# Branch sum on VectorE inside each attention-branch tile, earlier loads of the residual rows, and an unrolled output projection with the second norm and the first up tile woven in

## The chip, the cores and the metric

The kernel runs on one core of one Trainium2 chip. The metric is the device time of one execution in microseconds, and the figure quoted is a median over runs. The kernel before takes 1816.24 us (three runs, 1814.94 to 1818.01).

## The reference

One inference step of a decoder layer over 1024 prompt tokens and 8 x 4 sample tokens (1056 rows in all), all in float32. What matters here is the middle of it:

```
h = rmsnorm(x, g_mix_pre); z = h @ w_in            # pooling branch A, attention branch B, two gates
merged = gates[:D] * (pool_out @ w_branch_pool) + gates[D:] * (attn @ w_branch_attn)
x  = x + rmsnorm(merged @ w_out, g_mix_post)       # output projection, post norm, residual
up = rmsnorm(x, g_ffn_pre) @ ffn_w_up              # second norm, then the feed-forward
c  = causal depthwise conv of width 3 over [history, up]
x  = x + rmsnorm((gelu(c[:D_FF]) * c[D_FF:]) @ ffn_w_down, g_ffn_post)
```

D is 1024 and D_FF 2816. Each layer also returns its updated states (pool rows, key and value caches, convolution history).

## The kernel before

The program is written out engine by engine, with semaphores; each engine does its instructions in the order in which they are written, and so do the two queues that issue transfers (SyncE, shown as SPq, and GpSimd's). Nothing is scheduled by a planner.

**Products.** Every float32 product is three passes of TensorE: operands are split into a high part (a copy on ScalarE into a rounded type) and a low part (a subtraction on VectorE), and hi*hi, hi*lo and lo*hi are summed in PSUM. So each weight slice needs a load, a ScalarE copy and a VectorE subtraction before TensorE may use it.

**Layout.** In the projections of the input, of branch B and of the up matrix, channels lie on partitions and the 1056 tokens are three blocks of 352 columns (`BW`). In the output projection the tokens lie on partitions: nine tiles of 128 tokens, each 8 chunks x 3 passes x 2 halves of 512 columns, so 48 matmuls a tile.

**Around the change**, in order of time:
- Branch B's projection (L928 to L947): eight tiles j of 18 matmuls into banks 0 to 2 and 3 to 5 by turns. For tile j VectorE multiplies PSUM by the gate into `sga` (L1653), then makes `wo_lo` for slice j of w_out (L1655). GpSimd adds `sga` to `merged` (L690) and raises `sum_done`. SyncE loads the eight slices of w_out through four buffers `wo_stage` (L568); a buffer is loaded again when its `wo_lo` is done.
- SyncE then waits for all eight `wo_lo` and all eight sums, and issues the residual rows (`xnat`, two loads of 2 MB and two small ones, `load_x`, L441 to L444), the two gains `gpost` and `gb2` (L573, L575; the trace calls the second one gb), and the first weights of the up-projection (L507).
- Output tiles (`out_tile`, L952 to L962): tile n needs `mg_hi` and `mg_lo` of its tokens and, for its PSUM banks, the residual of tile n - 2. ScalarE (`split_merged`, `post_norm`, L1230 to L1245) makes `mg_hi`, squares and sums the PSUM tile into `pjunk`, takes the root, and squares the new `xnat` row. VectorE (`low_merged`, `residual`, L1661 to L1676) makes `mg_lo`, the reciprocal, `ptmp` and the new `xnat`. Six tiles run in loops of two; before its loop VectorE waits for both gains and all of `xnat`.
- Second norm: after tile 7, VectorE takes the reciprocals and scales two rows into `hn2` (L1360), in two buffers. TensorE transposes them (`turn_tiles`, L722 to L737, 8 transposes a tile), ScalarE and VectorE copy the result into `hT_hi` (L1041) and `hT_lo` (L1368), which lie over `wo_hi` and `wo_lo`. Only when all nine tiles are through does GpSimd clear `chist` (L693), after which SyncE loads the convolution history (L586), TensorE transposes it (L984) and starts up tile 0 (`channels`, L825 to L833: 72 matmuls for each of two halves).
- The up-projection has 22 such pairs of halves, then follows the down-projection (L1011).

## Time and profile before

| | |
|---|---|
| device time, median of 3 runs | 1816.24 us |
| span of the profiled execution | 1810.3 us |
| TensorE busy in it | 1655.2 us, 91% |
| VectorE, ScalarE, GpSimd busy | 730.4, 580.0, 184.6 us |
| branch B projection | 807.1 to 831 us |
| output tiles | 841.4 to 949.5 us |
| transposes of the second norm | 954.1 to 977.2 us |
| first half of up tile 0 | 981.0 to about 994.1 us |

The profile gives the span from the first to the last instruction. The profiled execution's own device time is not listed apart: the three runs lie 4.6 to 7.7 us above the span, and that difference, taken here as what lies around the span, is assumed to stay. The granted clock of TensorE is written as a share of 2.4 GHz, so 0.50 is 1.2 GHz.

### The profile page before, as it was taken

What the parts mean: (1) busy time and instruction counts of PE and PEld (TensorE: products, weight loads), DVE (VectorE), ACT (ScalarE), POOL (GpSimd) and SP (SyncE); (2) the same over time, 40 slices, a digit from 0 to 9 for tenths busy, and PEclk for the clock granted to TensorE, in tenths of its full rate; (3) what the DMA queues carried; (4) which work ended last, traced back from release to release, by engine and by line L of the source; (5) the groups of instructions that cost most, each with busy time, mean ns of one, the idle gap of its engine ahead of it and who ended that gap; (6) DMA issues with size and microseconds to landing.
All of it is one profiled execution on the core that took longest, in us unless ns stands there. A gap on an engine that the chain in (4) does not pass through costs nothing.

```text
span 1810.3 us, 26548 instructions
## 1 busy us (share of the span) xinstructions
PE 1655.2 (91%) x9651; PEld 1528.4 (84%) x9651; DVE 730.4 (40%) x1220; ACT 580.0 (32%) x1083; POOL 184.6 (10%) x223
## 2 busy tenths in 40 slices
PE   3999996776889999996996999999999999999996
PEld 2798895776889999995886999999999997878784
DVE  4424325563632223125344444334444344454533
ACT  5221214452322222232332333333333333343432
POOL 0011114444010000005000000000000000000000
PEclk8999997787889999998997999999999999999998
DMA  4232217776123332125002555555562114555542
GB/s 160 94 93 83 79 48 237 236 235 206 30 81 94 93 102 82 47 77 189 3 0 85 170 173 178 176 184 193 193 197 72 60 64 159 177 186 175 187 160 89
DMA packets 146747, 232.89 MB, mean 129 GB/s; under 512 B 13617, under 2 KB 114273, under 8 KB 145928
## 3 DMA queue, kind: packets, MB, share of 16 engines
q1 hardware_dynamic: 134944, 198.99, 34.7%
q0 software_dynamic: 11760, 33.35, 5.0%
q8 instruction: 25, 0.41, 0.1%
q14 instruction: 18, 0.15, 0.0%
HBM read 202.56 MB, written 77.36 MB: 155 GB/s over the span
## 4 chain that ended last, share of the span: by engine, by line
PE 79%; issue 6%; DMA 4%; DVE 3%; POOL 2%; SPq 2%; ACT 2%; POOLq 0%; DVEq 0%; ACTq 0%
PE PS L832 44%; PE PS L1011 14%; PE PS L753 11%; PE PS L959 5%; PE PS L892 2%; POOL merged L690 1%; SPq L520 1%; DMA gb<-in_norm_ffn_pre 1%; PE PS L731 1%; DMA qb<-zs 1%; DVE hn L1360 1%; SPq L515 1%; PE PS L808 1%; POOL qb L665 1%; ACT junk L1049 1%
## 5 line engine op out<-in xcount | busy, mean ns | idle before, releaser
L832 PE MATMUL PS<-hT_hi,tw_hi 128*128 128x352 f32 x1536 | 346.2, 334 | 16.8 <-DVE poolT_lo L1534 7.9
L832 PE MATMUL PS<-hT_hi,tw_lo 128*128 128x352 f32 x1536 | 338.0, 328 | 0.0
L832 PE MATMUL PS<-hT_lo,tw_hi 128*128 128x352 f32 x1536 | 337.9, 329 | 0.0
L832 PEld LDWEIGHTS PS<-hT_hi,tw_hi 128*128 128x128 f32 x1536 | 267.2, 195 | 19.0 <-issue 7.9
L1493 DVE TENSOR_TENSOR tw_lo<-tw_stage,tw_hi 128x1024 fp32r<-128x1024 f32 x74 | 86.2, 1167 | 464.1 <-ACT tw_hi L1140 460.3
L832 PEld LDWEIGHTS PS<-hT_hi,tw_lo 128*128 128x128 f32 x1536 | 270.1, 193 | 0.0
L832 PEld LDWEIGHTS PS<-hT_lo,tw_hi 128*128 128x128 f32 x1536 | 267.9, 193 | 0.0
L1140 ACT ACTIVATE tw_hi<-tw_stage 128x1024 fp32r<-128x1024 f32 x74 | 74.7, 1012 | 263.5 <-PE PS L832 248.9
L1716 DVE TENSOR_TENSOR wd_lo<-wd_stage,wd_hi 128x1024 fp32r<-128x1024 f32 x66 | 80.9, 1225 | 154.1 <-ACT as_hi L1274 153.3
L1739 DVE SCALAR_TENSOR_TENSOR cacc<-cext,cols,cacc 128x1024 f32<-128x1024 f32 x88 | 113.0, 1285 | 65.3 <-ACT cacc L1295 30.3
L1011 PE MATMUL PS<-wd_hi,as_hi 128*128 128x512 f32 x396 | 125.9, 399 | 9.9 <-DVE ytmp L1780 8.1
L1273 ACT ACTIVATE wd_hi<-wd_stage 128x1024 fp32r<-128x1024 f32 x66 | 69.9, 1059 | 176.7 <-PE PS L1011 168.1
L1011 PE MATMUL PS<-wd_lo,as_hi 128*128 128x512 f32 x396 | 124.0, 394 | 0.0
L1011 PE MATMUL PS<-wd_hi,as_lo 128*128 128x512 f32 x396 | 123.8, 394 | 0.0
L1011 PEld LDWEIGHTS PS<-wd_hi,as_hi 128*128 128x128 f32 x396 | 75.1, 192 | 28.3 <-DVE ytmp L1780 10.1
L1011 PEld LDWEIGHTS PS<-wd_lo,as_hi 128*128 128x128 f32 x396 | 75.5, 191 | 16.9
L1011 PEld LDWEIGHTS PS<-wd_hi,as_lo 128*128 128x128 f32 x396 | 75.2, 190 | 16.5
L753 PE MATMUL PS<-wqk_hi,hT_hi 128*128 128x512 f32 x216 | 86.2, 399 | 2.3 <-DVE wqk_lo L1389 2.3
L753 PE MATMUL PS<-wqk_hi,hT_lo 128*128 128x512 f32 x216 | 85.6, 396 | 0.0
L753 PE MATMUL PS<-wqk_lo,hT_hi 128*128 128x512 f32 x216 | 85.3, 395 | 0.0
L1304 ACT ACTIVATE cnat<-PS 18x256 f32<-18x256 f32 x22 | 8.2, 372 | 182.7 <-PE PS L977 182.7
L665 POOL TENSOR_TENSOR qb<-kt,qb 128x1024 f32<-128x1024 f32 x24 | 56.4, 2353 | 64.2 <-DMA qb<-zs 64.0
(235 smaller groups left out, 2361.8 us busy)
## 6 DMA issues: line engine op xcount, KB each, us to landing
wd_stage<-in_ffn_w_down SPq DMA_DIRECT2D x66, 512.0 KB, 3.3
tw_stage<-in_ffn_w_up SPq DMA_DIRECT2D x44, 512.0 KB, 3.9
out_k_s<-in_cache_k_w SPq DMA_DIRECT2D x8, 2044.0 KB
out_v_s<-in_cache_v_w SPq DMA_DIRECT2D x8, 2044.0 KB
qb<-zs SPq DMA_DIRECT2D x24, 512.0 KB, 5.8
acts<-cact POOLq DMA_DIRECT2D x22, 528.0 KB, 8.6
tw_stage<-in_w_in SPq DMA_DIRECT2D x20, 512.0 KB, 5.1
as_stage<-acts SPq DMA_DIRECT2D x44, 192.0 KB, 3.3
```

Of the source, the lines that this page charges most:

```text
L515: sp.dma_start(srow[h:P:NH, g, :, :], zs_s[g, h]).then_inc(s_rows_in, 16)
L665: pool.tensor_tensor(qb[s][:, :, :], k, qb[s][:, :, :], ALU.mult).then_inc(s_prod, 1)
L753: last = pe.matmul(PS[:, bank + n % 3, 0:width], x[:, k, t0:t0 + P], w[:, k, :], start=(k == 0 and j == 0), stop=(k == KC - 1 and j == 2))
L832: last = pe.matmul(PS[:, 3 * s + b, 0:BW], w[s][:, k, :], x[:, k, b * BW:(b + 1) * BW], start=(k == 0 and j == 0), stop=(k == kc - 1 and j ...
L892: last = pe.matmul(PS[0:DH, 6, bass.ds(r + g * P, 1)], vt[g][:, t, h * DH:(h + 1) * DH], sPT[:, g, bass.ds(r, 1)], start=True, stop=True)
L959: last = pe.matmul(PS[:, 2 * s + b, :], x[s][:, k, :], w[:, k, b * 512:(b + 1) * 512], start=(k == 0 and j == 0), stop=(k == KC - 1 and j ...
L1011: mm = pe.matmul(PS[:, 2 * pair + b, :], x[s][:, t0:t0 + P], w[s][:, b * 512:(b + 1) * 512], start=(first and j == 0), stop=(last and j == 2))
L1140: act.activation(tw_hi[s][:, 0:kc, :], tw_stage[s][:, 0:kc, :], ACT.Copy).then_inc(tw_hi_done, 1)
L1273: act.activation(wd_hi[s][:, :], wd_stage[s][:, :], ACT.Copy)
L1493: dve.tensor_tensor(tw_lo[s][:, 0:kc, :], tw_stage[s][:, 0:kc, :], tw_hi[s][:, 0:kc, :].bitcast(F32), ALU.subtract).then_inc(tw_lo_done, 1)
L1716: dve.tensor_tensor(wd_lo[s][:, :], wd_stage[s][:, :], wd_hi[s][:, :].bitcast(F32), ALU.subtract)
L1739: dve.scalar_tensor_tensor(acc[j + 1][:, 0:TP], e[:, lag:lag + TP], w, acc[j][:, 0:TP], ALU.mult, ALU.add)
```

## The change

It does five things.
1. The sum `merged + sga` moves from GpSimd to VectorE, right behind the multiplication of the same tile. Only three of the eight `wo_lo` stay among these tiles (after j = 3, 5 and 6); the other five come after `mg_lo` of tile 0.
2. SyncE issues the first 2 MB of the residual rows between slices 6 and 7 of w_out, as soon as branch B's matmuls are done, then `gpost` (after five sums) and `gb2` (after eight), and the other rows when all `wo_lo` are done. VectorE waits for each part of `xnat` at tiles 0, 4 and 8.
3. ScalarE splits tile 0 of `merged` before the last slice of w_out.
4. The loops over output tiles are written out. ScalarE takes a root per tile for the second norm too, and VectorE scales row n directly behind the residual of tile n, into `merged`, whose columns are free by then (tile 8 into `hn2_last`). TensorE transposes tile 0 behind output tile 7 and tile 1 behind output tile 8.
5. The first half of up tile 0 runs block by block (`up_first`): from the transposes of tile 4 on, three matmuls of block 0 follow each tile's transposes, then the rest of block 0 and blocks 1 and 2. The transposes of the history stand behind it.

```diff
         @block.sync
+                if k == 6:
+                    sp.wait_ge(tp_done[1], PAIR_BA + 1)
+                    load_x(0)
+            sp.wait_ge(sum_done, 5)
+            sp.dma_start(gpost[:, :], ...).then_inc(gain_in, 16)
+            sp.wait_ge(sum_done, KC)
+            sp.dma_start(gb2[:, :], ...).then_inc(gain_in, 16)
             sp.wait_ge(wo_lo_done, KC)
-            sp.wait_ge(sum_done, KC)
-            for a in range(3):
-                load_x(a)
...
+            load_x(1)
+            load_x(2)
         @block.gpsimd
-            for j in range(KC):
-                pool.wait_ge(ba_used, j + 1)
-                pool.tensor_tensor(merged[:, j, :], merged[:, j, :], sga[:, j, :], ALU.add).then_inc(sum_done, 1)
         @block.tensor
             out_tile(0, 0, True)
-            with pe.Fori(0, 4) as i:
-                out_tile(i * 2 + 1, 1)
-                out_tile(i * 2 + 2, 0)
-            pe.wait_ge(o_x2, 9 + 2)
-            turn_tiles(1, hn2)
-            pe.wait_ge(ht_done[1], 9 + 2)
+            for n in range(1, NTILE):
+                out_tile(n, n % 2)
+                if n >= 7:
+                    turn_second(n - 7)
+            pe.wait_ge(tw_lo_done, PAIR_UP * 2 + 1 + 2)
+            def up_first(b, k):
+                for j, (w, x) in enumerate(((tw_hi, hT_hi), (tw_hi, hT_lo), (tw_lo, hT_hi))):
+                    mm = pe.matmul(PS[:, b, 0:BW], w[0][:, k, :], x[:, k, b * BW:(b + 1) * BW], ...)
+                return mm
+            for n in range(2, NTILE):
+                turn_second(n)
+                if n == 4:
+                    pe.wait_ge(ht_done[1], 3 + 2)
+                    pe.wait_ge(o_x2, 9 + 2)
+                if n >= 4:
+                    up_first(0, n - 4)
+            for k in range(5, KC):
+                up_first(0, k)
+            for b in range(1, NBLK):
+                pe.wait_ge(ht_done[1], (3, 6, 9)[b] + 2)
+                for k in range(KC):
+                    last = up_first(b, k)
+            last.then_inc(tp_done[0], 1)
...
-            up(0, True)
+            turn_history(0)
+            channels(PAIR_UP, 1, KC, hT_hi, hT_lo, conv0[1], 0)
             up(1)
         @block.scalar
             split_merged(0, 0, 0)
+            split_wo(KC - 1)
+            for n in range(NTILE - 1):
+                split_merged(n + 1, (n + 1) % 2, LAST if n + 1 == 8 else (n + 1) * P)
                 act.wait_ge(ss_done, n + 9 + 1)
+                post_square(n)
+                second_square(n)
+                if n == 5:
+                    split_tw(PAIR_UP, 0, KC)
+                    split_tw(PAIR_UP, 1, KC)
+            act.wait_ge(ss_done, 8 + 9 + 1)
+            post_square(8)
+            split_turned(1, 0)
+            split_turned(1, 1)
+            second_square(8)
+            for n in range(2, NTILE):
                 split_turned(1, n)
         @block.vector
                 dve.tensor_tensor(g, PS[:, 3 * (j % 2):3 * (j % 2) + 3, 0:BW], g, ALU.mult).then_inc(ba_used, 1)
-                dve.wait_ge(wo_hi_done, j + 1)
-                dve.tensor_tensor(wo_lo[:, j, :], wo_stage[j % 4][:, :], wo_hi[:, j, :].bitcast(F32), ALU.subtract)\
-                   .then_inc(wo_lo_done, 1)
+                dve.wait_ge(ba_used, j + 1)
+                dve.tensor_tensor(merged[:, j, :], merged[:, j, :], sga[:, j, :], ALU.add).then_inc(sum_done, 1)
+                if j in (3, 5, 6):
+                    low_wo((3, 5, 6).index(j))
...
             low_merged(0, 0, 0)
+            for k in range(3, KC):
+                low_wo(k)
+            low_merged(1, 1, P)
             dve.wait_ge(gain_in, 48)
-            dve.wait_ge(x_in[0], 32)
-            dve.wait_ge(x_in[1], 32)
-            dve.wait_ge(x_in[2], 64)
...
+            for n in range(NTILE):
+                if n % 4 == 0:
+                    dve.wait_ge(x_in[n // 4], 64 if n == 8 else 32)
+                residual(n)
+                if n + 2 < NTILE:
+                    low_merged(n + 2, n % 2, LAST if n + 2 == 8 else (n + 2) * P)
+                if n == 6:
+                    low_tw(PAIR_UP, 0, KC)
+                    low_tw(PAIR_UP, 1, KC)
+                if n < 8:
+                    second_norm(n)
+            low(1, 0)
+            low(1, 1)
+            second_norm(8)
+            for n in range(2, NTILE):
                 low(1, n)
```

`turn_second(n)` is eight transposes of row tile n; `post_square`, `second_square`, `residual` and `second_norm` are the bodies of the old steps, one tile each; `residual` no longer waits for the residual before it.

How the instructions stand, at three places. First VectorE from tile 6 of branch B's projection to the output tiles (`sga` is the gated product, the numbers of `wo_stage` its four buffers, those of `mg_lo` the buffers of output tiles 0 and 1). Before:

```order
L1653 TENSOR_TENSOR sga<-PS,sga 128x1056
L1655 TENSOR_TENSOR wo_lo<-wo_stage_181,wo_hi 128x1024
L1653 TENSOR_TENSOR sga<-PS,sga 128x1056
L1655 TENSOR_TENSOR wo_lo<-wo_stage_182,wo_hi 128x1024
L1663 TENSOR_TENSOR mg_lo_185<-merged,mg_hi_183 128x1024
```

Now:

```order
L1690 TENSOR_TENSOR sga<-PS,sga 128x1056
L1692 TENSOR_TENSOR merged<-merged,sga 128x1056
L1681 TENSOR_TENSOR wo_lo<-wo_stage_181,wo_hi 128x1024
L1690 TENSOR_TENSOR sga<-PS,sga 128x1056
L1692 TENSOR_TENSOR merged<-merged,sga 128x1056
L1701 TENSOR_TENSOR mg_lo_185<-merged,mg_hi_183 128x1024
L1681 TENSOR_TENSOR wo_lo<-wo_stage_182,wo_hi 128x1024
L1681 TENSOR_TENSOR wo_lo<-wo_stage_179,wo_hi 128x1024
L1681 TENSOR_TENSOR wo_lo<-wo_stage_180,wo_hi 128x1024
```

The sum stands behind each product, the `wo_lo` behind tile 6 is that of slice 2 instead of slice 6, and those of slices 3 to 7 follow the first `mg_lo`.

Second, SyncE's queue at the same time, now:

```order
L568 DMA wo_stage_181<-in_w_out 128x1024
L441 DMA xnat<-in_x_prompt 128x4x1024
L568 DMA wo_stage_182<-in_w_out 128x1024
L573 DMA gpost<-in_norm_mix_post 128x1024
L575 DMA gb_190<-in_norm_ffn_pre 128x1024
L441 DMA xnat<-in_x_prompt 128x4x1024
```

and before:

```order
L568 DMA wo_stage_181<-in_w_out 128x1024
L568 DMA wo_stage_182<-in_w_out 128x1024
L441 DMA xnat<-in_x_prompt 128x4x1024 x2
L443 DMA xnat<-in_x_prompt 96x1024
L444 DMA xnat<-in_x_sample 32x1024
L573 DMA gpost<-in_norm_mix_post 128x1024
```

One half of the rows went ahead of the last slice of w_out, the other behind both gains.

Third, TensorE behind output tile 8 (`ident,hn` and `ident,merged` are transposes, `ident,chist` those of the history). Before:

```order
L731 MATMUL PS<-ident,hn_194 128x128 x8
L734 REGISTER_ALU
L734 COMPARE_AND_BRANCH
L731 MATMUL PS<-ident,hn_193 128x128 x8
L984 MATMUL PS<-ident,chist 128x128 x2
L832 MATMUL PS<-hT_hi,tw_hi_73 128x352 x3
L832 MATMUL PS<-hT_lo,tw_hi_73 128x352 x3
L832 MATMUL PS<-hT_hi,tw_lo_75 128x352 x3
```

Now:

```order
L958 MATMUL PS<-wo_hi,mg_lo_186 128x512 x2
L967 MATMUL PS<-ident,merged 128x128 x32
L978 MATMUL PS<-hT_hi,tw_hi_73 128x352
L978 MATMUL PS<-hT_lo,tw_hi_73 128x352
L978 MATMUL PS<-hT_hi,tw_lo_75 128x352
L967 MATMUL PS<-ident,merged 128x128 x8
```

The transposes of tiles 1 to 4 follow the last output tile, and behind those of tile 4 stand the first three matmuls of up tile 0 (L978 is `up_first`), where before the history's transposes and all of up tile 0 came last.

## Rows read from the trace of the kernel before

**Rows 1.** The page's first part: busy time, share of the span, instructions.
```profile
PE 1655.2 (91%) x9651; PEld 1528.4 (84%) x9651; DVE 730.4 (40%) x1220; ACT 580.0 (32%) x1083; POOL 184.6 (10%) x223
```

**Rows 2.** The chain of waits, in order of time: start, length, what.
```profile
811.77 27.14 POOL merged L690 x8
...
981.33 24.36 PE PS L832 x144
```

**Rows 3.** Timeline, branch B projection: start, length, engine, line, tiles [idle <-releaser].
```profile
810.13 0.64 PE L941 MATMUL PS<-attnT_hi,tw_hi 128*128 128x352 f32 x3
...
810.43 1.26 DVE L1653 TENSOR_TENSOR sga<-PS,sga 128x1056 f32<-128x1056 f32 x1 [3.35 <-PE PS L941]
...
811.60 1.22 DVE L1655 TENSOR_TENSOR wo_lo<-wo_stage,wo_hi 128x1024 fp32r<-128x1024 f32 x1
...
820.75 2.33 DVE L1655 TENSOR_TENSOR wo_lo<-wo_stage,wo_hi 128x1024 fp32r<-128x1024 f32 x1
...
824.68 0.65 PE L941 MATMUL PS<-attnT_hi,tw_hi 128*128 128x352 f32 x3
...
838.94 1.06 ACT L1232 ACTIVATE mg_hi<-merged 128x1024 fp32r<-128x1024 f32 x1 [11.36 <-POOL merged L690]
```

**Rows 4.** View of the tile merged: durations in ns min/median/max, first and last start.
```profile
L1663 DVE TENSOR_TENSOR mg_lo<-merged,mg_hi x9: 1217/1225/1227, 840.1 to 934.2; 128x1024 fp32r<-128x1024 f32 x9
...
L690 POOL TENSOR_TENSOR merged<-merged,sga x8: 3380/3429/3456, 811.8 to 835.5; 128x1056 f32<-128x1056 f32 x8
```

**Rows 5.** Timeline, output tiles 0 to 2.
```profile
841.42 1.19 PE L959 MATMUL PS<-wo_hi,mg_hi 128*128 128x512 f32 x2 [10.46 <-issue]
...
855.43 1.02 ACT L1237 ACTIVATE pjunk<-PS 128x1024 f32<-128x1024 f32 x1 [13.07 <-PE PS L959]
...
859.20 1.23 DVE L1663 TENSOR_TENSOR mg_lo<-merged,mg_hi 128x1024 fp32r<-128x1024 f32 x1 [17.88 <-DMA gb<-in_norm_ffn_pre]
...
860.48 1.22 PE L959 MATMUL PS<-wo_hi,mg_hi 128*128 128x512 f32 x2 [5.25 <-DVE mg_lo L1663]
```

**Rows 6.** DMA issues between 780 and 1010 us: KB each, median us to landing.
```profile
wo_stage<-in_w_out SPq DMA_DIRECT2D x8, 512.0 KB, 3.5
...
xnat<-in_x_prompt SPq DMA_DIRECT2D x2, 2048.0 KB, 12.2
...
gb<-in_norm_ffn_pre SPq DMA_DIRECT2D x1, 512.0 KB, 17.3
```

**Rows 7.** Stretches: busy (x) of PE, PEld, DVE, ACT, POOL; PEclk, DMA share, GB/s.
```profile
841.40:846.70 5.30, 5.28 (x13) 4.14 (x14) 0.00 (x0) 0.96 (x1) 0.00 (x0) 0.50 1.00 389
...
953.80:960.00 6.20, 4.02 (x18) 3.65 (x19) 2.85 (x3) 3.49 (x5) 0.00 (x0) 0.50 0.00 0
...
983.50:993.50 10.00, 10.00 (x63) 10.00 (x63) 0.00 (x0) 0.00 (x0) 0.00 (x0) 1.00 0.88 304
```

**Rows 8.** Timeline, last output tiles, transposes and first up-projection.
```profile
884.42 1.03 ACT L1237 ACTIVATE pjunk<-PS 128x1024 f32<-128x1024 f32 x1 [2.41 <-PE PS L959]
...
949.56 1.02 ACT L1237 ACTIVATE pjunk<-PS 128x1024 f32<-128x1024 f32 x1 [5.14 <-PE PS L959]
...
952.55 1.23 DVE L1676 TENSOR_TENSOR xnat<-xnat,ptmp 128x1024 f32<-128x1024 f32 x1
...
954.12 3.65 PE L731 MATMUL PS<-ident,hn 128*128 128x128 f32 x16 [4.59 <-DVE xnat L1676]
...
956.09 1.02 ACT L1041 ACTIVATE hT_hi<-PS 128x1024 fp32r<-128x1024 f32 x1 [0.80 <-PE PS L731]
...
957.15 1.23 DVE L1368 TENSOR_TENSOR hT_lo<-PS,hT_hi 128x1024 fp32r<-128x1024 f32 x1 [3.37 <-ACT hT_hi L1041]
...
965.16 1.09 PE L731 MATMUL PS<-ident,hn 128*128 128x128 f32 x8 [1.57 <-DVE hn L1360]
...
980.67 0.66 PE L984 MATMUL PS<-ident,chist 128*128 128x128 f32 x2 [3.46 <-issue]
...
994.15 1.06 ACT L1140 ACTIVATE tw_hi<-tw_stage 128x1024 fp32r<-128x1024 f32 x1 [16.52 <-PE PS L832]
```

More of the change, by code:

```diff
@@ L237, in build @@
         assert sb.end() <= V
-        hn2 = [at(Y + 4 * D * (1 + 2 * s))(f"hn2{s}", [P, D]) for s in range(2)]
+        hn2_last = at(Y + 3 * 4 * D)("hn2_last", [P, KC, P])
         CW_ = 2 + TP + NB * 6
@@ new lines, in post_square, with second_square @@
+                act.wait_ge(o_ss, n + 1)
+                act.activation(prms[:, 0, n:n + 1], pss[:, 0, n:n + 1], ACT.Sqrt, bias=eps[:, 0:1],
+                               scale=1.0 / D).then_inc(o_rms, 1)
+            def second_square(n):
+                act.wait_ge(o_x2, n + 1 + 2)
+                act.activation(pjunk[:, :], xnat[:, n, :], ACT.Square, accum_out=ss[:, 1, n:n + 1]).then_inc(ss_done, 1)
+                act.wait_ge(ss_done, n + 9 + 1 + 1)
+                act.activation(rms[:, 1, n:n + 1], ss[:, 1, n:n + 1], ACT.Sqrt, bias=eps[:, 0:1],
+                               scale=1.0 / D).then_inc(rms_done[1], 1)
@@ L1645, in _, with low_wo @@
             dve.wait_ge(sga_done, 4 + 1)
+            def low_wo(k):
+                dve.wait_ge(wo_hi_done, k + 1)
+                dve.tensor_tensor(wo_lo[:, k, :], wo_stage[k % 4][:, :], wo_hi[:, k, :].bitcast(F32), ALU.subtract)\
+                   .then_inc(wo_lo_done, 1)
             for j in range(KC):
@@ L1675, in residual, with second_norm @@
                 dve.wait_ge(o_step, n * 2 + 2)
-                dve.tensor_tensor(row, row, ptmp[:, :], ALU.add).then_inc(o_x2, 1)
+                dve.tensor_tensor(xnat[:, n, :], xnat[:, n, :], ptmp[:, :], ALU.add).then_inc(o_x2, 1)
+            def second_norm(n):
+                dve.wait_ge(rms_done[1], n + 1)
+                dve.reciprocal(rstd[:, 1, n:n + 1], rms[:, 1, n:n + 1]).then_inc(rstd_done[1], 1)
+                dve.wait_ge(rstd_done[1], n + 1)
+                if n == 8:
+                    dve.wait_ge(o_mm, NTILE + 2)
+                dst = hn2_last[:, :, :] if n == 8 else merged[:, :, n * P:(n + 1) * P]
+                dve.scalar_tensor_tensor(dst, xnat[:, n, :].rearrange("p (c d) -> p c d", d=P), rstd[:, 1, n:n + 1],
+                                         gb2[:, :].rearrange("p (c d) -> p c d", d=P),
+                                         ALU.mult, ALU.mult).then_inc(hn_ready[1], 1)
```

86 lines of the change are left out of this document (28 added, 58 removed).

## The prediction

> **What bounds the kernel now.** The page's first part [rows 1] has TensorE busy for 1655.2 of 1810.3 us, so only TensorE's idle or slowly clocked time can be won. The chain of waits tells where that is: from 981.33 on it is matmuls without a gap, 24.36 us for 144 of them, the pace of the whole up-projection; just before the output projection GpSimd's eight sums hold it for 27.14 us [rows 2]. The timeline shows three more places between 811 and 994 us, all in the code that the diff touches: TensorE waits 10.46 us before output tile 0, 5.25 us before tile 1 [rows 5], and from the last output tile (949.56) to the end of the first half of up tile 0 (994.15) 44.6 us pass [rows 8] for 72 transposes and 72 matmuls that take some 21 at full clock (nine times 1.09 [rows 8], and half of 24.36 less the cold start). Whatever ends the first half earlier moves all behind it by as much, because up and down run at TensorE's pace and their loads are issued by the same relative waits.
>
> **1. Branch B's sum, to the first output tile.** Each of the eight tiles takes TensorE (824.68 - 810.13) / 5 = 2.91 us [rows 3]. GpSimd takes 3.43 us per sum [rows 4] and ends last: ScalarE's `mg_hi` had waited 11.36 us for it and began at 838.94 [rows 3]. On VectorE, the multiplication takes 1.26 us at 1056 columns and `wo_lo` 1.22 at 1024 when GpSimd is idle, 2.33 when it adds at the same time [rows 3]; the nine `mg_lo`, of the same form and with GpSimd idle, all take 1.22 to 1.23 [rows 4]. So I price the sum on VectorE at 1.22 * 1056 / 1024 = 1.26 (bounds: 1.2 from `mg_lo`, 2.4 if 2.33 were the cost of the place and not of GpSimd; then the eight sums and three `wo_lo` would end at 846.7, and tile 0 would start 9 us later). I take the lower, since the row at 811.60 is the same instruction at the same place. The Trainium skill, SBUF — State Buffer, section "SBUF: two separate sides", says that VectorE with two SBUF inputs and GpSimd exclude each other for a whole instruction. By that rule, the trace agrees (1.22 against 2.33), and 1.26 holds now that GpSimd adds nothing; against it the sum below would be 9 us smaller.
> VectorE now needs 2.52 us a tile against TensorE's 2.91, plus 1.22 for `wo_lo` behind tiles 3, 5 and 6. Walked through from 810.43 [rows 3]: tile 3 starts at 819.05, `wo_lo` 0 ends 823.0, `wo_lo` 1 at 829.4, `wo_lo` 2 at 833.2, and the last sum at 835.8, 3 us earlier than GpSimd's. But ScalarE does `wo_hi` of slice 6 ahead of `mg_hi`, and slice 6 is issued only when `wo_lo` 2 is done: 833.2 + 3.5 to land [rows 6] + 1.06 = 837.8. Then `mg_hi` 1.06 and `mg_lo` 1.23: tile 0 starts at 840.3 instead of 841.42. **Gain 1.1 us** (bounds: 2.5 if slice 6 were no hindrance; -3 if the 2 MB of `xnat` issued right behind slow it).
> Slice 7 is the next to be late: its `wo_lo` 3 comes after `mg_lo` 0, so it is issued at 841.6, behind the 2 MB of `xnat` issued at 833.7. 3.5 us when alone, up to 17.3 as `gb2` had behind 5 MB [rows 6]. The two large loads landed in 12.2 us each by the median, two of them overlapping [rows 6], so one should be through in some 7 to 8, and I take 4.5: wo_lo 7 is done at about 849. Tile 0 took 14.0 us (841.42 to 855.43 [rows 5]), because TensorE starts it at half clock (granted 0.50 for 5.3 us [rows 7]); its last eighth begins some 12 us in, at 852.5. Hidden, with 3.5 us of cover.
>
> **2. Tile 1 and the pace.** Before, VectorE stood 17.88 us before `mg_lo` 1 because the gains and all of `xnat` came first, and TensorE stood 5.25 us [rows 5] and then ran at half clock again for 3.6 us (8 matmuls at 0.43 instead of 0.23: 1.6 us). Now `mg_lo` 1 stands ahead of that wait, done at about 850, 4 us before tile 0 ends. The gains (issued 842.6, 1.5 MB in the queue) should be there by 850; they are first wanted at 855.8. Tile 2 onwards: from one `pjunk` to the next 10.86 us pass, (949.56 - 884.42) / 6 [rows 8], all TensorE. ScalarE and VectorE need after a tile's end: square 1.2, root 0.3, reciprocal 0.2, `ptmp` 1.3, `xnat` 1.2 (949.56 to 953.78 with the pauses [rows 8]), second square and root 1.5, `mg_hi` 1.06, `mg_lo` 1.23, so 8.2 us, within 10.86; at n = 5 the two weight splits on ScalarE make it 10.3, still within. VectorE's second norm (0.2 + 1.3 a tile) fits beside it. So the tiles run gapless: 94.13 us from `pjunk` 0 to `pjunk` 8 [rows 5, 8] become 8 * 10.86 + 1.1 for tile 0's transposes (1.09 at full clock [rows 8]) = 88.0. **Gain 6.1 us.** Tile 8 ends at 942.2.
>
> **3. The tail.** The weights of up tile 0 are long there. From E = 942.2: square and root to +1.5, `hT_hi` 0 and 1 (1.02 each) to +3.6 on ScalarE; VectorE's residual of tile 8 ends at +4.2 as before, then `hT_lo` 0 and 1 (1.23 each [rows 8]) at +5.5 and +6.7. TensorE transposes tile 1 by +1, idles, and is cold at +5.6: the same pause of 4.59 us before 954.12 left the granted clock at 0.50 up to 960 [rows 7, 8]. Transposes of a tile then take 1.8 to 2.0 us (3.65 for two tiles [rows 8]). Tile 2 to +7.5, 3 to +9.5, 4 from +10.3 to +12.2 (waiting for `hT_lo` 2: second norm of tile 8 stands before it on VectorE). Then four times {three matmuls, transposes}: 0.5 + 1.1 at full clock, 0.9 + 2.0 at half; the loop transposes, `hT_hi`, `hT_lo` over two buffers holds it to (1.9 + 0.2 + 1.02 + 0.1 + 1.23) / 2 = 2.2. I take 2.4: tile 8's transposes end at +21.8. Left are 60 of the 72 matmuls, 0.162 each at full clock (11.66 for 72 in the steady pace, 24.36 for the first 144 [rows 2] less the cold start), 9.7 us: **E + 31.5**, so 973.7. Before it was 44.6 after E. **Gain 13.1 us**; the history's transposes now stand between the halves, where they cost 0.3 (0.66 for two when cold [rows 8]), and their load, before a wait of 3.46 us in the path (until 980.67 [rows 8]), lies under blocks 1 and 2 (GpSimd's memset at about 965, the data by 968). Bounds: all of the weave at half clock (transposes 2.0, matmuls 0.3 until block 1) gives 36; all at full clock 28.5.
> All else is moved, not changed: the down-projection, the cache copies, the last norms.
>
> **Sum.** 1.1 + 6.1 + 13.1 - 0.3 = 20.0 us off the profiled execution: its span goes from 1810.3 to 1790.3, and with what lies around it as before (5.9 us to the median), the median from 1816.2 to **1796.2**.
>
> **Rivals.**
> *The last slice of w_out is late* (10 in 100). If slice 7 takes the 17.3 us that `gb2` took, it lands at 858.9, `wo_lo` 7 at 861.3, and tile 0 stops for 8.5 us at its last eighth; TensorE restarts cold (1.6 us). Then 10 of the 20 us are lost: 1806. For it speaks that 2 MB lie ahead in the same queue; against it, that they have 8 us of start.
> *The tail stays cold* (10 in 100). A weave of short bursts with pauses keeps the clock at 0.50, and it needs 36 us or more instead of 31.5, or 39 with block 1 cold too: 1801 to 1804. The trace has both: 1.09 us for eight transposes at 965.16, 3.65 for sixteen at 954.12 [rows 8]. The Trainium skill, TensorE: Matmul & The Clock Gate, describes a kernel whose short pauses between groups of matmuls made the clock go back and forth, and counts a cost for each return; by that rule this rival is the likelier, and the pauses of the old transposes (0.50 from 953.8 to 960 [rows 7]) agree with it. It moves nothing in the sum, since my 2.4 us a step lies between both clocks.
> *VectorE does not get faster without GpSimd* (3 in 100): tile 0 starts 9 us later, 1805.
> *Slower than before* (4 in 100). Some 1150 TensorE instructions (48 matmuls and 48 weight loads a tile, transposes, weave) are now straight code where two loops ran; if the stream of instructions does not keep up, each tile stalls. It takes more than 20 us over nine tiles, 2.3 us a tile, to turn the sign; at 3 us a tile it would be 1796 + 27 = 1823. Against it: the 144 matmuls of branch B are straight code too and ran at 2.91 us a tile without such stalls [rows 3].
>
> **How the numbers follow.** The forecast as told has 73 in 100, with about 3 us to either side from the bounds; all rivals but the last also end faster. The cases between 1790 and 1805 hold about 84 in 100, and the late slice reaches to 1806, so the range is 1790.0 to 1805.0. A measurement tells about 0.2%, 3.6 us, from no change. Faster by more than that: 0.94 (all but the slower case and a late slice and cold tail together); within: 0.02; slower: 0.04.
>
> **What would show it.** In the profile of the changed kernel: sums on VectorE at 1.26 us, `wo_lo` at 1.22, first output matmul near 840, no idle of TensorE between output tiles 0 and 8, `pjunk` 10.9 us apart, 31.5 us from the last `pjunk` to ScalarE's next `tw_hi` (44.6 before), and all up halves at the old pace. Wrong would make it: a wait of TensorE for `wo_lo` in tile 0, granted clock 0.50 beyond the weave, `issue` gaps inside output tiles, or new waits for `tw_stage` in the first up tiles.

## The result and the profile after

The changed kernel takes **1789.51 us** (median of four runs, 1785.31 to 1799.03) beside 1817.12 us for the kernel before (four runs, 1814.94 to 1825.06): a ratio of 0.9856, with a 95% interval of 0.9818 to 0.9894. It is faster, by 26 us, where 20 were forecast; 1789.5 lies just below the range. The two repeats below, beside slightly slower runs of the kernel before, have 1792.23 and 1792.62 us, inside the range, and 27 to 28 us less than the kernel before.

The profiled execution is the slowest of the four, 1799.03 us with a span of 1797.4. In every run on record the device time is 1.6 to 1.7 us above the span. So what lies around the span is 1.7 us and not the 5.9 us of the prediction: by this the profiled execution of the kernel before took about 1812 us, some 4 less than its median. Its page begins, for the changed kernel:

```profile
span 1797.4 us, 26431 instructions
...
PE 1663.5 (93%) x9651; PEld 1538.1 (86%) x9651; DVE 734.9 (41%) x1235; ACT 575.0 (32%) x1085; POOL 157.3 (9%) x215
```

TensorE has the same 9651 matmuls as in [rows 1] and GpSimd is 27 us less busy, but TensorE's busy time has *grown* by 8 us and the span has shrunk by only 12.9. The windows view tells why, in a stage that the change does not touch (columns as in [rows 7]):

```profile
250.00:415.00 165.00, 133.52 (x935) 121.61 (x933) 81.39 (x284) 65.31 (x222) 69.70 (x58) 0.75 0.66 200
```

In these 165 us of the attention stage the kernel before was granted 0.80 of the clock and this execution 0.75, so branch B begins at 816.62 instead of 807.13. That alone is 9.5 us, and it comes and goes between runs of one and the same kernel (812.74 and 813.68 in the two repeats). So from here on I read a **stretch** inside one trace, with four marks: S, the first `sga` on VectorE in branch B; O, the first output matmul; P0 and P8, the first `pjunk` of output tiles 0 and 8; C, ScalarE's next `tw_hi`, which marks the end of up tile 0's first half. The marks of the changed kernel, from its timeline:

```profile
821.30 1.26 DVE L1690 TENSOR_TENSOR sga<-PS,sga 128x1056 f32<-128x1056 f32 x1 [4.74 <-PE PS L940]
...
849.83 1.19 PE L958 MATMUL PS<-wo_hi,mg_hi 128*128 128x512 f32 x2 [8.28 <-issue]
...
862.93 1.03 ACT L1268 ACTIVATE pjunk<-PS 128x1024 f32<-128x1024 f32 x1 [5.67 <-PE PS L958]
...
950.90 1.02 ACT L1268 ACTIVATE pjunk<-PS 128x1024 f32<-128x1024 f32 x1 [6.08 <-PE PS L958]
...
978.67 1.06 ACT L1170 ACTIVATE tw_hi<-tw_stage 128x1024 fp32r<-128x1024 f32 x1 [9.24 <-PE PS L978]
```

For the kernel before they are 810.43 [rows 3], 841.42 and 855.43 [rows 5], 949.56 and 994.15 [rows 8].

| us | S to O | O to P0 | P0 to P8 | P8 to C | S to C |
|---|---|---|---|---|---|
| before | 30.99 | 14.01 | 94.13 | 44.59 | 183.72 |
| after | 28.53 | 13.10 | 87.97 | 27.77 | 157.37 |
| gain | 2.46 | 0.91 | 6.16 | 16.82 | 26.35 |
| forecast | 1.1 | 0 | 6.1 | 13.1 | 20.3, less 0.3 behind C |

The stretch gives 26.35 us, the ratio 0.0144 * 1817 = 26.2. The profiled spans differ by 12.9, since 9.5 us went in the attention stage, 1.4 before S (TensorE entered branch B at half clock: 4.68 us from its first matmul to S instead of 3.30) and 2.6 behind C. From C to the end of the span are 816.2 us before and 818.7 here, and 816.7 and 818.6 in the repeats of the changed kernel, so 2 of the 2.6 come and go between runs of one kernel; I have not traced them further. The stretch of the kernel before comes from a single trace, and a near copy of that kernel, below, has one that is 4.1 us shorter.

The view of TensorE's waits from 813 to 990 shows what became of the four pauses:

```profile
PE PS L958 <- issue: 8.3, 1, 8.3
PE PS L967 <- DVE hT_lo L1400: 6.6, 4, 4.8
PE PS L940 <- DVE attnT_lo L1672: 2.4, 1, 2.4
```

The wait before output tile 0 is 8.3 instead of 10.46 us, the one before tile 1 is gone (both [rows 5]), and so is the 3.46 us wait for the history [rows 8]. In the transposes 4.8 us are left in one piece, about as long as before [rows 8], and 1.8 in three shorter ones. The third line is the entry into branch B, before the stretch. In the chain of waits the loops behind them are one piece, `849.83 89.18 PE PS L958 x384`, where the kernel before stopped after tile 0.

### The profile page after: what moved, and what is told of

Same layout as the page of the kernel before. It is cut to its first block, busy times and chain, and to the rows that moved or that the text cites. A ratio compares the mean times of both kernels' runs of the same rounds, so it can differ in the third digit from the quotient of the medians.

```text
span 1797.4 us, 26431 instructions
## 1 busy us (share of the span) xinstructions
PE 1663.5 (93%) x9651; PEld 1538.1 (86%) x9651; DVE 734.9 (41%) x1235; ACT 575.0 (32%) x1085; POOL 157.3 (9%) x215
## 4 chain that ended last, share of the span: by engine, by line
PE 81%; issue 7%; DVE 4%; DMA 3%; ACT 2%; SPq 2%; POOL 1%; POOLq 0%; DVEq 0%; ACTq 0%
PE PS L831 44%; PE PS L1039 15%; PE PS L752 11%; PE PS L958 6%; PE PS L891 2%; SPq L520 1%; PE PS L940 1%; DMA qb<-zs 1%; POOL qb L668 1%; SPq L515 1%; PE PS L978 1%; PE PS L807 1%; ACT junk L1079 1%; DMA tw_stage<-in_w_in 0%; DMA xnat<-in_x_prompt 0%
## 5 line engine op out<-in xcount | busy, mean ns | idle before, releaser
L831 PE MATMUL PS<-hT_hi,tw_hi 128*128 128x352 f32 x1512 | 341.2, 335 | 16.9 <-DVE poolT_lo L1566 7.9
L831 PE MATMUL PS<-hT_hi,tw_lo 128*128 128x352 f32 x1512 | 332.7, 328 | 0.0
L831 PE MATMUL PS<-hT_lo,tw_hi 128*128 128x352 f32 x1512 | 332.2, 328 | 0.0
L831 PEld LDWEIGHTS PS<-hT_hi,tw_hi 128*128 128x128 f32 x1512 | 263.2, 195 | 19.1 <-issue 7.8
L831 PEld LDWEIGHTS PS<-hT_hi,tw_lo 128*128 128x128 f32 x1512 | 265.6, 192 | 0.0
L831 PEld LDWEIGHTS PS<-hT_lo,tw_hi 128*128 128x128 f32 x1512 | 263.6, 193 | 0.0
```

The source lines that it names most:

```text
L831: last = pe.matmul(PS[:, 3 * s + b, 0:BW], w[s][:, k, :], x[:, k, b * BW:(b + 1) * BW], start=(k == 0 and j == 0), stop=(k == kc - 1 and j ...
```

## The experiments

Every ratio has its 95% interval; where intervals overlap, the verdict rests on the stretch. The kernel before was measured beside them in 9 to 13 runs on each chip used (medians 1819.0 to 1819.9).

### The changed kernel once more

> The change again, for a closer figure. If its gain is the three waits of the middle stage, the stretch from branch B's first matmul to the second half of up tile 0 is 162 us again (187 before), the total 25 us under before, and what varies between runs (1785 to 1799) lies in the attention stage, whose code is unchanged. If the further 7 us against my 20 are made elsewhere, another stretch is shorter than before by some us.

No edit. Measured 1792.23 us (1788.16 to 1795.55), ratio 0.9849 [0.9827, 0.9871]. From branch B's first matmul to C are 161.1 us, as expected. S to O 28.55, S to C 157.77: the stretch repeats within 0.4 us, while branch B begins at 812.74, four us earlier than in the first profile. ScalarE's and VectorE's rows settle the first rival, the late slice of w_out:

```profile
851.12 1.06 ACT L1255 ACTIVATE wo_hi<-wo_stage 128x1024 fp32r<-128x1024 f32 x1 [7.97 <-DMA wo_stage<-in_w_out]
...
852.21 1.23 DVE L1681 TENSOR_TENSOR wo_lo<-wo_stage,wo_hi 128x1024 fp32r<-128x1024 f32 x1 [3.19 <-ACT wo_hi L1255]
...
858.05 1.03 ACT L1268 ACTIVATE pjunk<-PS 128x1024 f32<-128x1024 f32 x1 [4.92 <-PE PS L958]
```

The last slice was issued at 845.64, behind 2 MB of rows, and ScalarE split it at 851.12, 5.5 us later; its `wo_lo` ended at 853.4, 4.6 us before tile 0 did. TensorE never waited for it.

### The sum back on GpSimd

```diff
 @block.gpsimd
+            for j in range(KC):
+                pool.wait_ge(ba_used, j + 1)
+                pool.tensor_tensor(merged[:, j, :], merged[:, j, :], sga[:, j, :], ALU.add).then_inc(sum_done, 1)
 @block.vector
-                dve.wait_ge(ba_used, j + 1)
-                dve.tensor_tensor(merged[:, j, :], merged[:, j, :], sga[:, j, :], ALU.add).then_inc(sum_done, 1)
```

> Only the eight sums go back to GpSimd. Theory: GpSimd ends them 27 us after the first product again, and output tile 0 starts 2 to 3 us later, total +2 to +3 us on the change, with wo_lo beside it at up to 2.3 us. Rival (the move of the sum is the main gain, as its 27 us in the chain suggest): +10 us or more. Rival (slice 6 of w_out sets the start anyway): no change.

Measured 1794.82 us (1787.95 to 1795.68), ratio 0.9866 [0.9848, 0.9884]; S to O **27.45**, 1.1 us *earlier* than with the sum on VectorE. So the expectation missed, and the rivals (10 us later, no change) missed too. A row of VectorE's, GpSimd's rows in the timeline, and its line in the view of the tile `merged`:

```profile
822.57 1.22 DVE L1685 TENSOR_TENSOR wo_lo<-wo_stage,wo_hi 128x1024 fp32r<-128x1024 f32 x1
```

```profile
814.11 2.46 POOL L693 TENSOR_TENSOR merged<-merged,sga 128x1056 f32<-128x1056 f32 x1 [29.04 <-DVE sga L1694]
816.91 2.46 POOL L693 TENSOR_TENSOR merged<-merged,sga 128x1056 f32<-128x1056 f32 x1 [0.34 <-DVE sga L1694]
...
822.73 14.97 POOL L693 TENSOR_TENSOR merged<-merged,sga 128x1056 f32<-128x1056 f32 x5 [0.44 <-DVE sga L1694]
```

```profile
L693 POOL TENSOR_TENSOR merged<-merged,sga x8: 2410/2466/3409, 814.1 to 835.3; 128x1056 f32<-128x1056 f32 x8
```

GpSimd needs 2.46 us for a sum, not 3.43 [rows 4]; it has pauses until VectorE's first `wo_lo` comes at 822.57, and ends the last sum 24.9 us after S. What made it late in the kernel before was a `wo_lo` beside every sum, not its own speed. And VectorE without the sums reaches `wo_lo` 2 sooner, so slice 6 arrives sooner (`wo_hi` 23.4 us after S, against 25.1 in the changed kernel): here the last sum holds `mg_hi`, there slice 6 does.

### The sum on VectorE, a weight split in every tile

```diff
-                if j in (3, 5, 6):
-                    low_wo((3, 5, 6).index(j))
+                low_wo(j)
...
-            for k in range(3, KC):
-                low_wo(k)
...
-                if k == 6:
+                if k == 7:
                     sp.wait_ge(tp_done[1], PAIR_BA + 1)
```

> The change, but with a wo_lo behind each of the eight sums as before (the first residual rows go behind slice 7). Theory: what starts output tile 0 earlier is not the sum's engine but the five wo_lo that left the tiles. VectorE then needs 1.26 + 1.26 + 1.22 = 3.74 us a tile, more than TensorE's 2.91, the last wo_lo ends some 33 us after branch B's first matmul, and the first output matmul comes at 35 to 36 us instead of 31.8 (34.3 before). Rival (the sum on VectorE is the gain): 32 to 33 us.

Measured 1800.72 us (1789.42 to 1803.78), ratio 0.9919 [0.9887, 0.9952]; S to O **32.26**, and 35.6 from branch B's first matmul, as expected. But the tiles are not all of it. Here too ScalarE makes `mg_hi` 0 before `wo_hi` of slice 7, while VectorE now has `wo_lo` 7 ahead of `mg_lo` 0, an order that neither kernel has:

```profile
843.75 1.04 ACT L1255 ACTIVATE wo_hi<-wo_stage 128x1024 fp32r<-128x1024 f32 x1
...
844.82 1.23 DVE L1681 TENSOR_TENSOR wo_lo<-wo_stage,wo_hi 128x1024 fp32r<-128x1024 f32 x1 [2.07 <-ACT wo_hi L1255]
```

`mg_hi` 0 was ready at 843.85, but `mg_lo` 0 began only at 845.97, behind slice 7. So S to O has to be parted at the end of the eighth sum, in us:

| | `wo_lo` among the tiles | S to the end of the eighth sum | from there to O | S to O |
|---|---|---|---|---|
| sum on GpSimd (before) | 8 | 28.48 | 2.51 | 30.99 |
| sum on VectorE (this run) | 8 | 27.73 | 4.53 | 32.26 |
| sum on GpSimd (the run above) | 3 | 24.93 | 2.52 | 27.45 |
| sum on VectorE (the change) | 3 | 24.43 | 4.10 | 28.53 |

`mg_hi` and `mg_lo` alone take the 2.5 us. Taking five `wo_lo` out of the tiles brings the eighth sum 3.3 to 3.5 us forward. The sum on VectorE, which gives the change its name, brings it forward by 0.5 to 0.75 us more, and yet output tile 0 starts 1.1 us *later* than with the sum on GpSimd, because slice 6 then stands in between (1.6 us). In this run it is slice 7 (2.0 us). Without it tile 0 would start about 27.7 + 2.5 = 30.2 us after S, an estimate, so these runs do not show that the sum on VectorE costs anything when all eight `wo_lo` stay.

With all three on VectorE a tile takes 1.26 + 1.26 + 1.22 us less their overlap, 3.6 from one `sga` to the next, against 2.91 on TensorE:

```profile
815.03 1.26 DVE L1690 TENSOR_TENSOR sga<-PS,sga 128x1056 f32<-128x1056 f32 x1 [3.36 <-PE PS L940]
816.33 1.26 DVE L1692 TENSOR_TENSOR merged<-merged,sga 128x1056 f32<-128x1056 f32 x1
817.50 1.22 DVE L1681 TENSOR_TENSOR wo_lo<-wo_stage,wo_hi 128x1024 fp32r<-128x1024 f32 x1
818.64 1.25 DVE L1690 TENSOR_TENSOR sga<-PS,sga 128x1056 f32<-128x1056 f32 x1
```

### Rows and gains late, as before

```diff
-                if k == 6:
-                    sp.wait_ge(tp_done[1], PAIR_BA + 1)
-                    load_x(0)
-            sp.wait_ge(sum_done, 5)
-            sp.dma_start(gpost ...)
-            sp.wait_ge(sum_done, KC)
-            sp.dma_start(gb2 ...)
-            sp.wait_ge(wo_lo_done, KC)
-            load_x(1)
-            load_x(2)
+            sp.wait_ge(sum_done, KC)
+            sp.wait_ge(wo_lo_done, KC)
+            for a in range(3):
+                load_x(a)
+            sp.dma_start(gpost ...)
+            sp.dma_start(gb2 ...)
```

> Only the loads are put back: all residual rows and then both gains behind the last wo_lo and the last sum. Theory: tile 0 and 1 still run, but gb2 lands some 18 us after the issue at about 857.6, so at 876, residual 0 comes 12 us late, and tile 2 stands for 6 to 7 us and starts at half clock: +8 us. Rival (mg_lo 1 ahead of the wait was all that mattered): within 1 us.

Measured 1804.77 us (1796.94 to 1809.09), ratio 0.9922 [0.9904, 0.9939]. The stretch is 167.09, 9.3 us longer, and all of it is at two tiles: 16.62 us from P0 to the next `pjunk` and 14.45 to the third, where the change has 10.88 and 10.88. The waits of TensorE and VectorE:

```profile
PE PS L954 <- DVE mg_lo L1697: 7.2, 1, 7.2
```

```profile
DVE prstd L1703 <- DMA gb<-in_norm_ffn_pre: 17.3, 1, 17.3
```

VectorE's 17.3 us before the reciprocal is the old 17.88 us before `mg_lo` 1 [rows 5], and behind it stand `residual` of tile 0 and `mg_lo` 2, so now tile 2 starts late. The early loads are worth 9.3 us, where 8 were expected, and the rival is false.

### No weave

```diff
             for n in range(2, NTILE):
                 turn_second(n)
-                if n == 4:
-                    pe.wait_ge(ht_done[1], 3 + 2)
-                    pe.wait_ge(o_x2, 9 + 2)
-                if n >= 4:
-                    up_first(0, n - 4)
-            for k in range(5, KC):
-                up_first(0, k)
-            for b in range(1, NBLK):
-                pe.wait_ge(ht_done[1], (3, 6, 9)[b] + 2)
+            pe.wait_ge(o_x2, 9 + 2)
+            pe.wait_ge(ht_done[1], 9 + 2)
+            for b in range(NBLK):
```

> Only the weave is undone: the first half of up tile 0 starts when all nine tiles are transposed. Theory: 12 matmuls and blocks 0 and 1 no longer hide under the transposes, 3.5 us later, and TensorE's clock may fall in the pauses, up to 8 us later in all. Rival (the gain of the tail comes from the norm being ready early, not from the weave): within 1.5 us of the change.

Measured 1793.57 us (1788.72 to 1795.2), ratio 0.9849 [0.9828, 0.9869]: by the medians no difference. By the stretch there is one, P8 to C 32.52 instead of 27.8, so the weave is worth 4.7 us, between the 3.5 and 8 of the expectation, and the rival is false. Twelve matmuls that the weave hides are 12 * 0.162 = 1.9 us, and the wait for the last `hT_lo` is 1.0. The rest is the clock, which falls again when the matmuls start (windows of 954.7 to 975):

```profile
954.70:961.20 6.50, 4.26 (x32) 3.43 (x32) 4.43 (x4) 3.54 (x4) 0.00 (x0) 1.00 0.00 0
962.20:965.60 3.40, 3.40 (x13) 3.40 (x14) 0.00 (x0) 0.00 (x0) 0.21 (x1) 0.54 0.09 25
966.00:975.00 9.00, 9.00 (x58) 9.00 (x57) 0.00 (x0) 0.00 (x0) 0.00 (x0) 1.00 0.36 100
```

TensorE was busy for 4.26 of the 6.5 us of transposes at a granted 1.00, and then got 0.54 for 3.4 us of gapless matmuls.

### The second norm late, as before

```diff
 @block.tensor
                 out_tile(n, n % 2)
-                if n >= 7:
-                    turn_second(n - 7)
+            turn_second(0)
+            turn_second(1)
 @block.vector
-                if n < 8:
-                    second_norm(n)
-            low(1, 0)
-            low(1, 1)
-            second_norm(8)
-            for n in range(2, NTILE):
-                low(1, n)
+            second_norm(0)
+            second_norm(1)
+            for n in range(NTILE):
+                low(1, n)
+                if n + 2 < NTILE:
+                    second_norm(n + 2)
```

> The second norm is put back behind the output tiles: VectorE scales rows 0 and 1 after the residual of tile 8 and each further row between two hT_lo, TensorE transposes tiles 0 and 1 behind tile 8; the weave stays. Theory: VectorE then needs 1.3 + 0.15 + 1.23 us for each of nine tiles behind tile 8, some 24 us against the 17 of the change, and sets the end of the tail: the first half of up tile 0 ends 5 to 7 us later than in the change (161 us after branch B's first matmul). Rival (TensorE's own 8 transposes a tile and its clock set the pace of the tail): within 1.5 us.

Measured 1801.04 us (1799.99 to 1808.54), ratio 0.9911 [0.9885, 0.9937]. P8 to C is 38.22 us; the stretch is 9.4 us longer than in the repeat of the change, where 5 to 7 were expected. TensorE waits for every row:

```profile
PE PS L967 <- DVE merged L1722: 12.0, 7, 5.8
```

```profile
949.22 3.68 PE L967 MATMUL PS<-ident,merged 128*128 128x128 f32 x16 [5.83 <-DVE merged L1722]
955.00 1.07 PE L967 MATMUL PS<-ident,merged 128*128 128x128 f32 x8 [2.10 <-DVE merged L1722]
957.48 1.97 PE L967 MATMUL PS<-ident,merged 128*128 128x128 f32 x8 [1.41 <-DVE merged L1722]
960.01 1.97 PE L967 MATMUL PS<-ident,merged 128*128 128x128 f32 x8 [0.55 <-DVE merged L1722]
963.22 1.33 PE L967 MATMUL PS<-ident,merged 128*128 128x128 f32 x8 [0.36 <-DVE merged L1722]
```

VectorE takes 2.5 us a row (scale 1.29, `hT_lo` 1.24), and the transposes of one tile read the clock: 1.07 us, then 1.97 and 1.97, and 1.33 on the way back. From the end of tile 8's residual to the end of tile 8's transposes 24.1 us pass, as forecast, but in the changed kernel (955.20 to 969.01) 13.8 and not 17, and that is the miss. The norm in the shadow of the output tiles is worth 9.4 us, as much as the early loads, against 4.7 for the weave.

### The kernel before with its loops written out

```diff
-                with pe.Fori(0, 4) as i:
+                for i in range(4):
...
-            with act.Fori(0, 3) as i:
+            for i in range(3):
...
-            with dve.Fori(0, 3) as i:
+            for i in range(3):
```

(The first line twice: branch A's and the output projection's loop on TensorE.)

> The kernel before with its loops over output tiles and transposes written out and nothing else. Theory: loops and branches cost nothing here, TensorE is not made to wait by either: from branch B's first matmul to the end of the first half of up tile 0 it stays 187 us, within 1 us (two table loads fewer on ScalarE lie beside matmuls). Rival (the stream of straight code is too slow): some us longer. Rival (part of the gain is the unrolling itself): 3 us or more shorter.

Measured 1812.62 us (1809.59 to 1820.56), ratio 0.9977 [0.9958, 0.9997]: straight code is not slower, and the rival that ended slower is false. The expectation missed all the same, since the stretch S to C is 4.1 us shorter (2.7 from branch B's first matmul, where TensorE entered at half clock). The pace is not what changed (10.88 us a tile). It is tile 1: TensorE's wait there is 3.4 us instead of 5.25, and the granted clock stayed at 1.00 behind it, where the kernel before had 0.50 for 3.6 us:

```profile
865.40 0.73 PE L959 MATMUL PS<-wo_hi,mg_hi 128*128 128x512 f32 x2 [3.42 <-DVE mg_lo L1663]
```

The view of DMA issues has the rows that the wait hangs on:

```profile
xnat<-in_x_prompt SPq DMA_DIRECT2D x2, 2048.0 KB, 10.4
...
gb<-in_norm_ffn_pre SPq DMA_DIRECT2D x1, 512.0 KB, 15.5
```

The gains landed after 15.5 us instead of 17.3 and the rows after 10.4 instead of 12.2 [rows 6]. Whether unrolling does that or one profile differs from another is open. For unrolling speak the medians, which give 4.2 us as well (0.5 to 7.6 by the interval), and the run with late rows above, also written out, which had 15.8 and 10.5; against it, that there is one profile of each. It is no further part of the gain: in the changed kernel this wait is gone, however long it was. Beside this run the changed kernel's stretch is 22.3 us shorter, instead of 26.35.

### Two steps further

The first is to free slice 6 earlier and take it off the path: only `wo_lo` 0 stays among branch B's tiles, the rows are issued behind slice 3, and ScalarE splits tile 0 ahead of slices 5 to 7.

```diff
-                if k == 6:
+                if k == 4:
                     sp.wait_ge(tp_done[1], PAIR_BA + 1)
...
-            for k in range(KC - 1):
+            for k in range(5):
                 split_wo(k)
...
-            split_wo(KC - 1)
+            for k in range(5, KC):
+                split_wo(k)
...
-                if j in (3, 5, 6):
-                    low_wo((3, 5, 6).index(j))
+                if j == 3:
+                    low_wo(0)
...
-            for k in range(3, KC):
+            for k in range(1, KC):
                 low_wo(k)
```

> A step further at the start: only wo_lo 0 stays among the products (behind tile 3), ScalarE makes mg_hi 0 before slices 5 to 7 of w_out, and the first residual rows are issued behind slice 4. Theory (VectorE's two wo_lo and ScalarE's wait for slice 6 set the start of output tile 0 in the change): first output matmul 28.6 us after branch B's first instead of 31.8, and all behind it 3 us earlier, unless slices 5 to 7 come late (each needed within 1 to 2 us of where I expect it): then 1 to 2 us of idle in tile 0. Rival (the eight sums themselves set the start): at most 0.5 us.

Measured 1794.09 us (1787.94 to 1794.97), ratio 0.9856 [0.9828, 0.9884], with the attention stage at 0.74 in its profile. S to O is 25.35, 3.2 us less than the change, S to C 154.45. From branch B's first matmul it is 28.6 us, as expected. VectorE's eighth sum ends 22.8 us after S here, and tile 0 starts 2.5 us behind it, with no slice in between; with the sum back on GpSimd it ended at 24.9. Even at 2.46 us a sum behind TensorE's 2.91 a tile GpSimd could not end before some 1.3 + 7 * 2.91 + 2.5 = 24.2. So by this estimate (no such kernel was run) the sum's place on VectorE is worth 1 to 1.5 us once no slice of w_out stands between the last sum and output tile 0.

The second is to let the tail begin before tile 8's norm: ScalarE and VectorE copy the transposes of tiles 0 and 1 ahead of tile 8's square and residual.

```diff
 @block.scalar
-            post_square(8)
             split_turned(1, 0)
             split_turned(1, 1)
+            post_square(8)
+            split_turned(1, 2)
+            split_turned(1, 3)
             second_square(8)
-            for n in range(2, NTILE):
+            for n in range(4, NTILE):
 @block.vector
+                if n == 8:
+                    low(1, 0)
+                    low(1, 1)
                 residual(n)
...
-            low(1, 0)
-            low(1, 1)
+            low(1, 2)
+            low(1, 3)
             second_norm(8)
-            for n in range(2, NTILE):
+            for n in range(4, NTILE):
```

> A step further in the tail: hT_hi and hT_lo of tiles 0 and 1 go ahead of the square and the residual of tile 8, and the second norm of tile 8 behind hT_lo 3. Theory (TensorE's idle 4.8 us behind the last output tile is the residual of tile 8 in VectorE's queue): the first hT_lo is ready 2.4 us after tile 8 instead of 5.6, TensorE stays at full clock, and the first half of up tile 0 ends 24 to 25 us after tile 8 instead of 27.8: -3 us. Rival: what is won at the first transposes is lost again where hT_lo 2 now stands behind the residual: within 1 us.

Measured 1788.77 us (1785.35 to 1792.23), ratio 0.9838 [0.981, 0.9867]; S to C 155.26, 2.5 less than the repeat of the change, where 3 were expected and the rival had at most 1. The clock stayed full, as the theory had it (window of 940 to 968):

```profile
940.00:968.00 28.00, 22.10 (x148) 20.27 (x147) 13.85 (x16) 11.22 (x15) 0.31 (x1) 1.00 0.14 39
```

> Both steps together. They lie in different places, so their gains add: the first half of up tile 0 ends 155 us after branch B's first matmul (161 in the change, 187 before), the time 6 us under the change and 33 under before.

Both together: 1788.42 us (1782.51 to 1790.92), ratio 0.983 [0.9801, 0.9859]; S to O 25.36, S to C 152.35. The two add up within 0.4 us: 5.4 us less than the repeat of the change. From branch B's first matmul it is 157.0 instead of 155, since TensorE entered branch B at half clock here, and the median is 31 us under the kernel before instead of 33. By the medians alone the second step and both together (1788.77 and 1788.42) are not told apart.

Then the change and both steps once more, side by side on one chip:

> The change once more, beside the version with both further steps, since the times of single runs differ by up to 14 us with the clock of the attention stage. From the first gated product to the end of the first half of up tile 0: 157.4 to 157.8 us as in its two traces so far.

> Both further steps again (output tile 0 earlier, first transposes earlier). The same stretch: 152.3 us as in its first trace, and a median 5 us under that of the change on the same chip. Rival (what the middle stage gains is given back later): the stretch is shorter, the median not.

Measured 1792.62 us (1789.07 to 1796.08), ratio 0.9846 [0.9829, 0.9862], for the change, and **1787.39 us** (1778.33 to 1788.73), ratio 0.9804 [0.978, 0.9828], for both steps. The intervals just part, and the stretches are 157.44 and 152.06. TensorE's waits in the latter:

```profile
PE PS L967 <- DVE hT_lo L1403: 5.8, 4, 2.7
PE PS L958 <- issue: 5.1, 1, 5.1
```

The wait before tile 0 is 5.1 us where the change has 8.3, and the longest in the transposes 2.7 where it has 4.8. This version beats both kernels, by about 5 us and 32 us.

## Why the prediction came out as it did

**What bounds the kernel** was right: the gain is TensorE's idle and half-clock time in the stretch, and both the ratio and the stretch give it as 26 us. The terms that missed (1.4, 0.9 and 3.7 us, as told below) all missed to the same side. The last line of the sum, 5.9 us from the span to the median, was called what lies around the span and is mostly a profiled execution faster than the median; since the 20 us are taken off both, the forecast of the median does not hang on that.

**Step 1, to the first output tile:** forecast 1.1 us, measured 2.46 in a range of -3 to 2.5. The prices held: sums at 1257 to 1259 ns, `wo_lo` at 1217 to 1228:

```profile
L1692 DVE TENSOR_TENSOR merged<-merged,sga x8: 1257/1258/1259, 822.6 to 844.5; 128x1056 f32<-128x1056 f32 x8
```

```profile
L1681 DVE TENSOR_TENSOR wo_lo<-wo_stage,wo_hi x8: 1217/1219/1228, 832.4 to 856.3; 128x1024 fp32r<-128x1024 f32 x8
```

So VectorE did get faster without GpSimd, and the rival that denied it is false. One row was misread on the way: the `wo_lo` at 811.60 was not done with GpSimd idle, since GpSimd's first sum began at 811.77 [rows 2, 3]; that 1.22 is the price without GpSimd is told by `mg_lo` [rows 4]. The walk said `wo_lo` 2 would end 22.8 us after S; it did after 22.0, since operations of VectorE overlap by up to 0.1 us at their ends (`wo_lo` starts 1.18 us after a sum of 1.26 does). Slice 6 took about 3.1 us instead of 3.5. The order was as told: slice 6, not the sum, held `mg_hi`:

```profile
844.47 1.26 DVE L1692 TENSOR_TENSOR merged<-merged,sga 128x1056 f32<-128x1056 f32 x1
...
846.39 1.06 ACT L1255 ACTIVATE wo_hi<-wo_stage 128x1024 fp32r<-128x1024 f32 x1 [2.46 <-DMA wo_stage<-in_w_out]
847.36 1.04 ACT L1264 ACTIVATE mg_hi<-merged 128x1024 fp32r<-128x1024 f32 x1
```

What the step did *not* see is which edit earns the gain. I priced the sum on VectorE against 3.43 us on GpSimd, and took 3.43 for GpSimd's own time, though the same paragraph held that the two engines hinder each other. The run with the sum back on GpSimd shows 2.46 and a start that is 1.1 us earlier; what earns the step is the five `wo_lo` that left the tiles.

**Step 2, tile 1 and the pace:** forecast 6.1 from P0 to P8, measured 6.16; every tile at 10.88 us without a wait, `mg_lo` 1 done at 858.7, 4.2 us before tile 0's end. That the early loads carry it was argued then and is shown now (9.3 us if undone). Tile 0 itself, taken as unchanged, gained 0.91 us (0.54 in the repeat, where it took 13.47); it has the same matmuls, and how long it stays at half clock differs from run to run of one kernel.

**Step 3, the tail,** is the term that was mis-sized: forecast E + 31.5, measured 27.8, below even the bound of 28.5. Up to the restart all was right (TensorE idle for 4.79 us, restart at +5.6). The chain of waits shows the rest:

```profile
956.47 1.96 PE PS L967 x8
958.45 1.03 ACT hT_hi L1071
959.51 1.24 DVE hT_lo L1400
...
960.88 1.08 PE PS L967 x8
961.99 1.03 ACT hT_hi L1071
963.04 1.24 DVE hT_lo L1400
...
964.41 1.08 PE PS L967 x8
...
967.94 1.07 PE PS L967 x8
969.01 9.55 PE PS L978 x60
```

From one buffer's transposes to its next, 960.88 to 964.41, are 3.53 us: transposes 1.08, `hT_hi` 1.03, `hT_lo` 1.24 and the handovers. Two tiles share it, so a step is 1.77 us. I had put the *half-clock* transposes (1.9) into that loop, got 2.2, and then taken 2.4 for caution. Tile 4's transposes ended at E + 11.1 instead of 12.2, and four steps at 0.63 less add 2.5: together 3.7 us, the whole difference. At full clock my own loop would have been (1.09 + 0.2 + 1.02 + 0.1 + 1.23) / 2 = 1.82. The windows show the clock that the step feared:

```profile
957.00:960.80 3.80, 2.94 (x15) 2.70 (x13) 3.04 (x4) 1.84 (x2) 0.00 (x0) 0.65 0.00 0
961.00:968.90 7.90, 6.98 (x53) 5.98 (x53) 5.70 (x5) 4.10 (x5) 0.00 (x0) 1.00 0.01 2
```

It was half while tiles 2 and 3 were transposed (3.47 us for the two), and full for the whole weave, in which TensorE was busy for 6.98 of 7.9 us. So the rival "the tail stays cold" is false here. It is not false of the hardware, though. The run with the late norm, where the transposes have pauses of 0.4 to 2.1 us between them, went from full to half clock and back, and the one without a weave went from 1.00 to 0.54 at 962. The Trainium skill, TensorE: Matmul & The Clock Gate, section "HAM oscillation — how this bites in real kernels", describes a kernel with waits of some 3 to 5 us between groups of matmuls, in which the clock falls and returns each time, at a cost. The run with the late norm agrees with it in the falling and returning, but its pauses are shorter than those, and the changed kernel, whose pauses inside the weave are 0.5 us, does not show it. The length of a pause alone does not part these runs: the kernel before with its loops written out kept 1.00 behind 3.4 us.

The history's transposes cost 0.22 us between the halves, where the forecast had 0.3.

**Slower than before** had four in a hundred; the stretch has no idle of TensorE inside an output tile, and unrolling the old kernel did it no harm.

## To carry to other kernels

When an engine looks too slow for its work, see what runs beside it before moving the work: here a sum on GpSimd took 3.43 us only because VectorE split a weight beside each, and putting off splits that nobody needed yet brought the last sum 3.3 to 3.5 us forward, where moving the sums brought 0.5 and lost 1.6 to a slice that came later. When an undoing run changes what stands between two marks, part the stretch there before its difference is put down to one edit. Price a loop over two buffers at both clocks and carry both values through, because a value between them is right at neither. And when a stage elsewhere moves the total by as much as the edit does, compare a stretch between fixed marks in the traces: the weave's 4.7 us could not be seen in the medians and can be in the stretch, which repeats within 0.4 us for the changed kernel.
